# Writing u to DRAM already regrouped, eight small transfers a tile from two queues, and loading a block of it with one

## The reference

```
proj = n @ w_in                      # 528 tokens x (z | xbc | dt | u)
u = proj[..., o_u:]                  # 528 x 1024: 64 groups of 16 channels
u = u.reshape(bsz, length, 64, 16)
bu = einsum('blgh,gph->blgp', u, bb)         # real and imaginary part, 64 states a group
s = associative_scan(combine, (a, bu))       # along the tokens
y = einsum('blgp,ghp->blgh', s, c) + u * d_skip
y = gelu(y) ... GLU, norm, w_out, MLP, second block
```

## Time and profile before

| | |
|---|---|
| median of 3 executions | 2878.06 us (2877.31, 2878.06, 2886.95) |
| the profiled execution | 2879.68 us, its span 2877.9 us |
| mean granted TensorE clock | 0.983 |
| busy share of the span | PE 97%, PE weight load 79%, DVE 53%, POOL 45%, ACT 38% |

### The profile page before, as it was taken

How to read it: one execution, slowest core, us unless ns; L and a number is a source line. 1 busy time by engine, 2 the same in 40 slices (tenths; PEclk the granted TensorE clock), 3 DMA queues, 4 the chain that set the end, 5 groups by cost and what they waited for, 6 DMA issues and landing times.

```text
span 2877.9 us, 41299 instructions
## 1 busy us (share of the span) xinstructions
PE 2780.8 (97%) x15766; PEld 2286.9 (79%) x15766; DVE 1516.4 (53%) x1961; ACT 1084.4 (38%) x1666; POOL 1304.2 (45%) x752
## 2 busy tenths in 40 slices
PE   7998987999999999999999999999999999999998
PEld 7975745878888878877788888888887778888887
DVE  7866686453324255268865432423455887452535
ACT  4435223433323233245543422322343554342433
POOL 3434323535435174388843332232347894354443
PEclk9999988999999999999999999999999999999999
DMA  5246296323323244432221221212233223233332
GB/s 188 94 164 254 93 322 200 110 81 111 95 87 102 90 125 131 145 101 91 67 88 59 81 65 59 65 60 66 67 95 117 89 66 96 73 102 95 95 102 73
DMA packets 109735, 306.88 MB, mean 107 GB/s; under 512 B 29008, under 2 KB 37328, under 8 KB 109072
## 3 DMA queue, kind: packets, MB, share of 16 engines
q1 hardware_dynamic: 87728, 284.95, 31.0%
q10 hardware_dynamic: 19504, 16.19, 1.9%
q0 software_dynamic: 2352, 3.67, 0.4%
HBM read 294.95 MB, written 7.45 MB: 105 GB/s over the span
## 4 chain that ended last, share of the span: by engine, by line
PE 87%; DVE 4%; issue 2%; POOL 2%; DVEq 1%; ACT 1%; DMA 1%; SPq 0%; ACTq 0%; POOLq 0%
PE ps L296 41%; PE ps L330 17%; PE ps L321 6%; PE ps L1963 3%; PE ps L1959 3%; PE ps L1964 3%; PE ps L1967 3%; PE ps L2376 2%; POOL wlo L257 2%; PE ps L2036 1%; PE ps L2017 1%; PE ps L749 1%; PE ps L2005 1%; DVE nacc L443 1%; PE ps L2007 1%
## 5 line engine op out<-in xcount | busy, mean ns | idle before, releaser
L257 POOL TENSOR_TENSOR wlo<-wraw,whi 128x1024 fp32r<-128x1024 f32 x373 | 924.7, 2489 | 1275.1 <-ACT whi L249 1272.7
L249 ACT ACTIVATE whi<-wraw 128x1024 fp32r<-128x1024 f32 x373 | 391.9, 1055 | 455.0 <-PE ps L296 169.9
L296 PE MATMUL ps<-xah,whi 128*128 128x512 f32 x992 | 387.9, 391 | 1.7 <-issue 1.7
L296 PE MATMUL ps<-xal,whi 128*128 128x512 f32 x992 | 387.4, 391 | 0.0
L296 PE MATMUL ps<-xah,wlo 128*128 128x512 f32 x992 | 280.1, 391 | 0.0
L2262 DVE SCALAR_TENSOR_TENSOR co<-ub,vec,co 128x512 f32<-128x512 f32 (+1 forms) x216 | 254.2, 1216 | 4.7 <-issue 0.7
L296 PEld LDWEIGHTS ps<-xah,whi 128*128 128x128 f32 x992 | 186.0, 188 | 42.8 <-issue 2.7
L296 PEld LDWEIGHTS ps<-xal,whi 128*128 128x128 f32 x992 | 186.1, 188 | 40.3
L296 PEld LDWEIGHTS ps<-xah,wlo 128*128 128x128 f32 x992 | 186.1, 188 | 40.2
L2363 POOL TENSOR_TENSOR co<-co,ct 128x512 f32<-128x512 f32 (+1 forms) x144 | 165.6, 1150 | 20.5
L296 PE MATMUL ps<-hhi,whi 128*128 128x512 f32 x408 | 159.3, 390 | 0.0
(11 more groups left out here) (418 smaller groups left out, 6003.6 us busy)
## 6 DMA issues: line engine op xcount, KB each, us to landing
wraw<-stream SPq DMA_DIRECT2D x425, 512.0 KB, 3.5
wada<-w_ada SPq DMA_DIRECT2D x96, 512.0 KB, 7.1
biasb<-attn_bias ACTq DMA_DIRECT2D x32, 256.0 KB, 3.4
xin<-x0T SPq DMA_DIRECT2D x4, 528.0 KB, 6.8
s_u<-uk ACTq DMA_DIRECT2D x8, 264.0 KB, 3.8
res<-x0T ACTq DMA_DIRECT2D x1, 2048.0 KB, 14.2
outT<-res SPq DMA_DIRECT2D x4, 512.0 KB, 2.6
s_y<-yk POOLq DMA_DIRECT2D x56, 32.0 KB, 5.2
```

The lines of the kernel that those rows point to most:

```text
L249: act.activation(whi[:, s], wraw[:, s], ACT.Copy).then_inc(hi_done[s], 1)
L257: pool.tensor_tensor(wlo[:, s], wraw[:, s], whi[:, s].bitcast(F32), ALU.subtract).then_inc(lo_done[s], 1)
L296: last = pe.matmul(ps[:, bank, 0:b - a], w[:, s, kt], x[:, kt, c0 + a:c0 + b], start=start, stop=stop)
```

## The change

ACT no longer stores a tile of u with one transfer. It is cut into eight, one for each group g of 16 channels, each 16 partitions of 8 runs of 264 B; ACT's queue issues g = 0 to 3, POOL g = 4 to 7. The DRAM tile is now written as S5 reads it, row 16k+h with (g, c) behind it, so that `s5_load` is one transfer of 128 rows of 2112 B. A second pair of semaphores, `s_ux`, counts POOL's transfers, and all who waited for the store wait for both. POOL's loop over the units of u is written out in `proj_pool`: for each tile it waits for ACT's copy, issues four transfers, and then makes the `wlo` of unit m+4.

```diff
+    s_ux = [sem(f"s5_u_written_by_pool{b}") for b in range(2)]
...
+    def u_out(eng, m, g):
+
+        return eng.dma_start(ud[m].rearrange("(k h) (g c) -> g h k c", k=LB, g=8)[g], uk[16 * g:16 * g + 16, m % 2])
+
+    def proj_pool(pool):
+        for m in range(NT):
+            pool.wait_ge(acc_free[(U_U + m) % R], read_out(U_U + m))
+            for g in range(4, 8):
+                u_out(pool, m, g).then_inc(s_ux[m % 2], 16)
+            split_lo(pool, U_U + m + R)
...
             if m >= 2:
-                act.wait_ge(s_uw[m % 2], 16 * (m // 2))
+                act.wait_ge(s_uw[m % 2], 64 * (m // 2))
+                act.wait_ge(s_ux[m % 2], 64 * (m // 2))
...
             act.wait_ge(acc_free[s], read_out(U_U + m))
-            act.dma_start(ud[m], uk[:, m % 2].rearrange("p k c -> p (k c)")).then_inc(s_uw[m % 2], 16)
+            for g in range(4):
+                u_out(act, m, g).then_inc(s_uw[m % 2], 16)
...
     def ssd_dve(dve):
 
         for b in range(2):
-            dve.wait_ge(s_uw[b], 16 * (NT // 2))
+            dve.wait_ge(s_uw[b], 64 * (NT // 2))
+            dve.wait_ge(s_ux[b], 64 * (NT // 2))
...
-        for k in range(LB):
-            sp.dma_start(u3[i % 3][16 * k:16 * k + 16], ud[i].rearrange("(g h) (k c) -> k h g c", g=8, k=LB)[k]).then_inc(s_u3[i % 3], 16)
+        sp.dma_start(u3[i % 3].rearrange("p g c -> p (g c)"), ud[i]).then_inc(s_u3[i % 3], 16)
...
-        pe.wait_ge(s_u3[i % 3], 128 * (i // 3 + 1))
+        pe.wait_ge(s_u3[i % 3], 16 * (i // 3 + 1))
...
-            pool_units(pool, U_U, 2)
+            proj_pool(pool)
```

More of the change, by code:

```diff
@@ L2845, in _ @@
             for b in range(2):
-                sp.wait_ge(s_uw[b], 16 * (NT // 2))
+                sp.wait_ge(s_uw[b], 64 * (NT // 2))
+                sp.wait_ge(s_ux[b], 64 * (NT // 2))
             for i in range(2):
```

## The result

Before took 2883.47 us at the median of 20 executions, the changed kernel 2891.86 us (20 executions too). The ratio is 1.0032, with a 95% interval of 1.0021 to 1.0042: 6 to 12 us slower. That is small, but it is outside the forecast range, and a cost where the forecast had none.

A forecast was written before the change was run, and what follows sets the result against it. PE, busy for 97% of the span, was taken as the bound. The projection's terms cost 0 and S5 gained 0.5 us: 2879.68 minus 0.5 makes 2879.2, or 2877.6 us against the runs, range 2870 to 2888.

The forecast's parts named there:

- POOL's issues: Projection: four issues take 2.1 us ahead of each split; cost 0, thinnest cover 2.9 us at unit 4.
- The copies' wait: Projection: ACT's copies wait for all eight transfers of tile m-2; cost 0, cover 6.2 us.
- sign of being wrong: Prediction is wrong if PE waits for a `whi` or `wlo` before 100 us, or S5 shortens by over 8 us.
- ACT's four issues: Projection: at 0.622 us each, four take 2.5 us between ACT's copies; cost 0, cover 4.9 us.
- DMA work: Projection, 46 to 82 us: small stores add a net 126 us of engine time, share 0.54 to about 0.76; nothing added.
- S5: S5 stage: one load replaces eight, `wada` loads can go 3.9 us earlier, but PE paces them; 0.5 us gained.
- Rival 3: S5 is paced by its DMA after all: six blocks by 3.9 us, 23 us faster, 2855 us; chance 0.06.
- Rival 2: Projection: small stores land late, in 12.5 us, delaying ACT's copies: +10 us, 2888 us; chance 0.07.
- Rival 1: Projection: POOL becomes the pacer through long issues (1.6 us each) beside DVE: +20 us, 2898 us; chance 0.05.

The follow-up runs named there:

- e9: Kernel before, POOL without stores, with DVE making the second S5 power table three times instead of once ahead of the dt step: 2892.27 us, ratio 1.003.
- e1: Changed kernel with POOL's 32 small stores on SP's queue instead, POOL's loop as before: 2884.66 us, ratio 0.9999 against the kernel before.
- e3: Changed kernel with DVE's `powers` step moved from ahead of the dt step to behind the convolutions: 2885.16 us, ratio 1.0002 against the kernel before.
- e5: Kernel before with only S5's load changed to one transfer a block, stores as before: 2886.05 us, ratio 0.9998.
- e2: Changed kernel with a POOL drain between its four small stores and the split: 2900.3 us, ratio 1.0063 against the kernel before.
- e8: Changed kernel with POOL doing the split first and the tile's four small stores after it: 2886.44 us, ratio 1.001 against the kernel before.
- e6: Changed kernel with all eight small stores of a tile on ACT's queue, POOL's loop as before: 2885.29 us, ratio 1.0006 against the kernel before.
- e4: Kernel before plus POOL's 32 small stores ahead of its splits, into a tensor nothing reads, copies waiting for them: 2894.66 us, ratio 1.0037.

## Why the prediction was wrong

**The step that failed** is "POOL's issues", with its "Cost 0, cover 2.9 us". Its list of what queues behind them was "the split, PE that waits for it ... and SP that reloads the raw slot", and DVE was not in it. The trace of before had it already. DVE's operations beside splits in the same stretch were held for some 2.1 us each (2.62 us for the pair that takes 0.46). That DVE was busy for 32.17 of 36 us was read as work, while about half of it was waiting at POOL: eight operations together took 16.7 us more than the same forms take where no split stands beside them. The last sentence of "The copies' wait" comes to the right place, "ACT waited 7.90 us for DVE at the next step", and reads it as cover for ACT. It was a sign that DVE's queue is the late one there: whatever DVE loses ahead of the dt step moves ACT's high half of unit 13 by the same amount.

**The term in its right form.** 32 issues of 0.528 us stand ahead of splits, 16.9 us in all, and DVE's dt step came 11.4 us later (91.05 to 102.4). Before, PE ended unit 12 at 102.42 + 2.10 = 104.5 us and the high half of unit 13 was done at 96.00 + 1.04 = 97.04, a cover of 7.5 us. With the change PE was there at 108.46 - 4.16 = 104.3 us, 0.2 earlier. 11.4 + 0.2 less 7.5 is 4.1, the gap of 4.16. This is the same two traces added up and no test of the cause. The clock adds 2.9. The prediction priced this at nothing, where the traces show 7.1 us and the ratio 9.2. Its sign of being wrong, a wait of PE "before 100 us", also stopped just short of the place. e9, e1 and e3 make the cause shown, from all sides: DVE late without POOL's stores loses the time, the stores without POOL lose none, and with POOL's stores kept, but less of DVE's work ahead of the dt step, nothing is lost.

**What was right.** POOL's own arithmetic: four issues took 2.08 us (forecast 2.1), the first split that has them ahead ended at 52.9 us (forecast 53.0), and no unit waited for a low half. ACT's four issues took a median of 0.454 us each (taken: 0.622). ACT's copies waited 13.1 us in four places for stores that landed in 1.7 to 6.4 us (3.8 median), without a gap on PE, as the tile's rows show against the earlier trace rows:

```profile
L644 ACTq DMA_DIRECT2D s_u<-uk x32: 309/454/1387, 47.9 to 80.5; - x32
L644 POOL DMA_DIRECT2D s_u<-uk x32: 528/528/712, 48.2 to 81.6; - x32
...
  DMA s_u<-uk: 13.1, 4
...
DMA to landing us min/median/max: 1.7/3.8/6.4
```

**DMA work** came out at 0.65 of the time from 46 to 82 us, against 0.54 before and a forecast of 0.76, so too high by half of the addition. The queues from 50 to 82 us (packets, MB, share of 16 engines; POOL's queue is q0):

```profile
q10 hardware_dynamic: 4168, 0.98, 18.1%
q0 software_dynamic: 884, 0.95, 12.0%
```

A small store on ACT's queue costs 18.1% x 16 x 32 / 29 = 3.2 us of one engine's time (taken: 2.7), one of POOL's 2.1 (taken: 3.9).

**S5** was right in its result. One load a block, landing in 3.8 to 11.6 us, and nothing gained (e5: 0.9998). SP's wait for PE at the `wada` loads rose from 33.7 us to 65.6, more than the 20 us forecast, as it should if PE paces them. Rival 3 falls with it.

**The rivals.** Rival 2 (stores land late) didn't come: the slowest store landed in 6.4 us. Rival 1 looked at the right pair of engines in the wrong direction: it asked whether DVE slows POOL's issues. In the changed kernel they took 0.528 us, but the DVE beside them was mostly waiting. e2 settles it: four issues took 2.09 us (56.12 to 58.21) beside DVE operations that ran at their normal 0.23 to 0.53 us a row. So DVE doesn't slow them, here. It is POOL that keeps DVE out. The Trainium skill, page "SBUF — State Buffer", section "Who interferes with whom", says that the two share a port pair by an exclusive lock on which the loser blocks fully, and its section "SBUF: two separate sides" counts a VectorE operation with two SBUF inputs against a GpSimd operation that reads SBUF. The rows of the splits agree: the operation from 66.37 us ended at 70.74, the split at 70.68. The same page of the Trainium skill also says that whichever starts first gets the pair. The row from 66.37 us differs: that DVE operation started 1.9 us ahead of the split's recorded start (68.27) and still lost to it, and the measurement decides. Whether the split took the pair ahead of its recorded start, or the first start doesn't count, no run here tells apart.

**Still open.** What in POOL's queue shuts DVE out. e2 and e8 show that issues without a ready split don't, and issues with one do. From what instant is not settled. In the changed kernel ACT's row

```profile
70.62 1.06 ACT L249 ACTIVATE whi<-wraw 128x1024 fp32r<-128x1024 f32 x1
```

puts a high half at 71.68 us, and a DVE operation that started 0.8 us after it, at 72.47, still went through; the next one, at 72.77, was held. In e8 one that started 0.45 us after the high half did not get through (64.25 against 63.80). The 2.1 us between the 7.1 us of the traces and the 9.2 of the ratio aren't placed, and lie within its interval. e9, which has the old layout, has as much (5.5 us in its trace, 8.7 by its ratio), so the new layout isn't needed for it.

## What to carry to other kernels

An operation of GpSimd that reads SBUF and VectorE's operations with two inputs there are one resource in this kernel: before work is put on GpSimd's queue, price it for VectorE as well, and follow VectorE's queue to the next step that somebody waits for. A wait for an engine is cover only for the engine that waits; for the one that is waited for, it says that there is no slack. If small stores must go on GpSimd, put them behind the tensor operation and not ahead of one that is ready (e8), or give the queue of another engine a try (e1, e6).

## What the runs showed of the hardware

- Four small stores take 2.08 us to issue on POOL, but the drain behind them ended only 4.59 us later (e2; 2.7 to 5.0 in its other rounds), with DVE running at its normal pace in all that time.
- DVE's busy time includes its wait for POOL: an operation of 0.23 us is recorded with 4.37 us, and of the 32.17 us that DVE was busy from 46 to 82 us before the change, 16.7 were such waiting (against the same forms with no split beside them).
- One gap of 4.16 us on PE is followed by 8 us (108 to 116) at a granted clock of 0.50, then 0.70, and costs 2.9 us more than itself; gaps of 3.74 (e9) and 5.79 us (e4) cost 1.8 and 2.6 more.
